# Output projection of both mixers in three rounded products per tile, with the splitting of its weights inside the attention

## The chip, the cores and the metric

The kernel runs on one core of a Trainium2 chip. Its time is the device time of one execution in microseconds (us); of several executions the median is given. The profile comes from one execution, and its times are counted from the first instruction in it.

## The reference, cut to what matters

Two decoder layers over 256 tokens of width 1024. Each layer has a token mixer (layer 0: sparse attention in three branches with gates; layer 1: causal block attention), a residual with LayerNorm, a mixture of 16 experts (top 2 of one group of 4), and a residual with LayerNorm again. The change touches the product with `w_out` at the end of each mixer:

```
def nsa_mixer(h, w_in, w_out, ...):
    proj = h @ w_in
    ...
    o = g[:, :, 0] * heads(o_cmp) + g[:, :, 1] * heads(o_slc) + g[:, :, 2] * heads(o_win)
    return o.reshape(B, S, D_MODEL) @ w_out          # (256 x 1024) @ (1024 x 1024)

def moba_mixer(h, w_in, w_out):
    ...
    o = lax.map(chunk, jnp.arange(S // QB))
    return _merge_chunks(o) @ w_out

for layer in range(2):
    mix = nsa_mixer(x, ...) if layer == 0 else moba_mixer(x, ...)
    x = layer_norm(DN_ALPHA * x + mix, ...)
    x = layer_norm(DN_ALPHA * x + grouped_moe(x, ...), ...)
```

All of it is fp32. The kernel has two ways to multiply at that precision: a plain fp32 matmul, or three matmuls in fp32r (a rounded fp32), in which each factor is split into its rounded value (hi) and the rest (lo), and hi x hi, hi x lo and lo x hi are added up.

## The kernel before, in words

Each engine has its own program, and semaphores tie them together. The weights stream from memory by SyncE's queue into `ring`, eight slots of 128 x 4096 fp32 (2 MiB each); a ninth place is `extra`, a part of `R56`. A slot is loaded anew when TensorE has used what was in it.

**Projections** (`project`, lines 478 to 498, and `split_hi`, `split_lo`). A unit of weights is 1024 x 512, in one slot, cut into eight chunks of 128 x 512, j = 0 to 7. For each chunk ScalarE casts it to fp32r (line 901, into `wh`), VectorE subtracts that from the chunk (line 1155, into `wl`), and TensorE does three fp32r matmuls for each of the two token tiles a (lines 492 to 494). `xh` and `xl` hold the split input.

**Attention** (`attention`, lines 596 to 614) goes by items m, 16 in layer 0 and 8 in layer 1; an odd item has 256 keys for each query, an even one 128. One item passes from engine to engine: TensorE's scores (lines 525, 529, 534), VectorE's maximum (`attention_max`, line 1204), ScalarE's four exponentials with their sums (line 1027), VectorE's coefficient (`coefficients`, line 1237 and in layer 0 also 1242), GpSimd's scaling of the probabilities (line 1100), TensorE's transposes (line 548), VectorE's copy of them out of PSUM (line 1419), TensorE's product with the values (`times_v`, line 564), and after every second item VectorE's copy of the output into `OT` (line 1428 in layer 0, 1430 in layer 1). The order on each engine is written out by hand: VectorE's loop (lines 1410 to 1430) does in turn the maximum of item m, the coefficient of m-1, the copy of the transposes of m-2, and in odd turns from m = 5 on the copy to `OT`. TensorE's does the scores of m, the transposes of m-2 and the values of m-3. ScalarE does the exponentials of m (lines 1018 to 1030), GpSimd the scaling of m (lines 1098 to 1100).

**Output projection** (`mix_out`, lines 616 to 627). The two units of `w_out`, w = 0 and 1, lie in two ring slots. Each of 8 chunks j, 2 token tiles a and 2 units w is one fp32 matmul of 128 x 128 by 128 x 512, 32 in each layer; in the profile an fp32 matmul is two MATMUL records, so line 623 has 128. The order is (a, w) = (0,0), (0,1), (1,0), (1,1). The first six of (0,0) stand before the values of the last item, the others behind. The residual was put into the PSUM banks before (`seed`, line 630). After (0,1) comes the LayerNorm of token tile 0 on VectorE, beside TensorE's (1,0); in the middle of (1,1) stand the logits of the router (line 636). SyncE waits with the next expert loads for (1,0) and (1,1), which free the slots of `w_out`.

**Experts** (`experts`, lines 713 to 764) are fp32 matmuls against weights from the ring (lines 678 and 699), pair by pair; they keep SyncE's queue full.

Of the kernel before, what the change touches and what calls it, by code (L numbers as in the profile page):

```python
# [15 lines left out]
P = 128  # L16
D, S = 1024, 256
T = S // P
# [72 lines left out]
def build(nc, x, consts, w_in0, w_out0, cmp_kw1, cmp_kw2, cmp_vw1, cmp_vw2, cmp_kpos, cmp_vpos,  # L91
          w_in1, w_out1, router_w, router_b, w_gate, w_up, w_down, ln_g, ln_b, out):
    ctx = ExitStack()
    with ctx:
        def sb(name, shape, dt=F32):
            return ctx.enter_context(nc.sbuf_tensor(name, shape, dt))

        def sem(name):
            return ctx.enter_context(nc.semaphore(name))


        ring = sb("ring", [P, SLOT, KJ * UNIT])
        wh = sb("wh", [P, WBUF, UNIT], F32R)
        wl = sb("wl", [P, WBUF, UNIT], F32R)
# [1 line left out]
        X = sb("X", [P, T, D])  # L106
        xh = sb("xh", [P, KJ, S], F32R)
        xl = sb("xl", [P, KJ, S], F32R)
        R2 = sb("R2", [P, T * D])
        R3 = sb("R3", [P, T * D])  # L110
        R4 = sb("R4", [P, T * D])
        R56 = sb("R56", [P, 6 * D])
        R5, R6 = R56[:, 0:3 * D], R56[:, 3 * D:6 * D]
        extra = R56[:, 2 * D:6 * D]
        small = sb("small", [P, 832])
# [18 lines left out]

        qT = R2[:, :].rearrange("p (j t) -> p j t", j=KJ)
        OT = [R6[:, 1536 + j * S:1536 + (j + 1) * S] for j in range(6)] + [R5[:, 2560 + j * S:2560 + (j + 1) * S] for j in range(2)]
        OT2 = [R6[:, 1536 + u * 512:2048 + u * 512] for u in range(3)] + [R5[:, 2560:3072]]
        xTr = R3[:, :].rearrange("p (j t) -> p j t", j=KJ)
        Xp = [v[:, :, :].rearrange("p j t -> p (j t)").rearrange("p (a j c) -> p a j c", a=T, j=KJ) for v in (xh, xl)]
# [61 lines left out]
        landed = [[sem(f"landed{s}_{h}") for h in range(2)] for s in range(SLOT + 1)]  # L201
        w_hi, w_lo, w_used = sem("w_hi"), sem("w_lo"), sem("w_used")
        cmpw_used = sem("cmpw_used")
        bconst = sem("bconst")
        out_done = sem("out_done")
        padded, round_over = sem("padded"), sem("round_over")
# [15 lines left out]
        def ready(k, t, w):  # L222
            return 2 * (k * T + t) + w + 1
# [43 lines left out]
        def in_slot(what):  # L267
            n = SLOT_OF[AT[what]]
            return ring[:, n] if n < SLOT else extra

        def landing(what, h):
            c = AT[what]
            n = sum(1 for b in range(c + 1) if SLOT_OF[b] == SLOT_OF[c] and (h == 0 or in_halves(STREAM[b])))
            return landed[SLOT_OF[c]][h], 16 * n
# [49 lines left out]
        def out_of(l, u, b):  # L324
            return ps[:, 6 + u % 2, 0:S] if l == 0 else ps[:, 6 + u % 2, b * S:(b + 1) * S]


        block = ctx.enter_context(nc.Block())

# [136 lines left out]
        def _(pe):  # L466
# [148 lines left out]

            def mix_out(l, a, w, js):
                B, u = base[l], OUT[2 * l + w]
                for j in js:
                    if a == 0 and w == 0:
                        pe.wait_ge(L.ot_sb, B.ot_sb + j + 1)  # L620
                    if a == 0 and j % 4 == 0:
                        pe.wait_ge(*landing(("unit", u), j // 4))
                    last = mm(ps[:, 2 * a + w, :], OT[j][:, a * P:(a + 1) * P],  # L623
                              in_slot(("unit", u))[:, j * UNIT:(j + 1) * UNIT],
                              start=False, stop=(j == KJ - 1), skip_group_check=True)
                if j == KJ - 1:
                    last.then_inc(L.mix, 1)

# [260 lines left out]
        def _(act):  # L889
# [67 lines left out]
            for l in range(2):  # L957
# [60 lines left out]
                for m in range(n):  # L1018
                    act.wait_ge(L.mx, B.mx + m + 1)
                    if m >= 2 and m % T == 0:  # L1020
                        act.wait_ge(L.pt, B.pt + m - 1)
                    if m >= 4 and m % T:
                        act.wait_ge(L.pt, B.pt + m - 3)
                    k = (m % T + 1) * P
                    for a in range(2):
                        for b in range(2):
                            last = nc.scalar.activation(probs(m)[:, a, b], ps[:, 2 * (m % T) + a, b * k:(b + 1) * k], ACT.Exp,  # L1027
                                                        bias=nmax[:, m % 2, a, b:b + 1],
                                                        accum_out=sums[:, m % 3, a, b:b + 1])
                    last.then_inc(L.exp, 1)  # L1030
                    if l == 0 and m == 1:
                        act.wait_ge(c_less, 1)
                        nc.scalar.activation(Pc, Pc, ACT.Exp).then_inc(c_exp, 1)
                def rows_hi(a, w):
                    c = slice(64 * w, 64 * w + 64)
                    act.wait_ge(N.x_ready, ready(2 * l, a, w))
                    copy(Xp[0][:, a, :, c], X[:, a].rearrange("p (c j) -> p j c", j=KJ)[:, :, c]).then_inc(R.xp, 1)

                for a in range(T):
# [17 lines left out]
        def _(pool):  # L1057
# [29 lines left out]
            for l in range(2):  # L1087
# [10 lines left out]
                for m in range(ITEMS[l]):  # L1098
                    pool.wait_ge(L.coef, B.coef + m + 1)
                    tt(probs(m), probs(m), bc(coef[:, m % 3], 3, (m % T + 1) * P), ALU.mult).then_inc(L.scaled, 1)  # L1100
                for k in (2 * l, 2 * l + 1):
                    for t in range(T):
                        pool.wait_ge(N.stats, k * T + t + 1)
                        tt(rstd[:, t:t + 1], ve[:, t:t + 1], half[:, t:t + 1], ALU.pow).then_inc(N.rstd, 1)
                        if k == 2 * l:
                            for w in range(2):
                                c = slice(64 * w, 64 * w + 64)
                                pool.wait_ge(R.xp, C.xp + 2 * t + w + 1)
                                tt(Xp[1][:, t, :, c], X[:, t].rearrange("p (c j) -> p j c", j=KJ)[:, :, c],
                                   Xp[0][:, t, :, c], ALU.subtract).then_inc(R.xl, 1)  # L1110
                    if k == 2 * l:
                        pool.wait_ge(R.table, C.table + 1)
                        experts(l)
                        pool.wait_ge(R.over, C.over + 1)
                        most = pool.value_load(over[0:1, 0:1], min_val=0, max_val=S)
                        with pool.If(most > SLOTS):
                            pool.wait_ge(main.comb, 2 * T * PAIRS * (l + 1))
                            with pool.Fori(0, ROUNDS - 1) as rho:
                                spare_round(spare[l], rho)
                                pool.wait_ge(spare[l].comb, 2 * T * PAIRS * (rho + 1))  # L1120
                                pool.sem_inc(round_over, 1)
# [3 lines left out]
        def _(dve):  # L1125
# [245 lines left out]
            for l in range(2):  # L1371
# [38 lines left out]
                for m in range(n + 4):  # L1410
# [10 lines left out]
                        compressed_scale()  # L1421
                    if l == 0 and m == 3:
                        compressed_copy()
                    if m >= 4 and m % T:
                        dve.wait_ge(L.pv, B.pv + m - 3)
                        u = (m - 4) // T
                        if l == 0:
                            copy(OT[u], ps[:, 6 + u % 2, 0:S]).then_inc(L.ot_sb, 1)
                        else:
                            copy(OT2[u], ps[:, 6 + u % 2, :]).then_inc(L.ot_sb, 2)  # L1430
                half_stats(0, 0, 0, L.mix, B.mix + 1)
                step(half_stats(0, 1, 0, L.mix, B.mix + 2))
                layer_norm(2 * l, 0, 0, L.ln_in, B.ln_in + 32)
# [63 lines left out]
```

## Time and profile before

| | us |
|---|---|
| median of 3 runs | 785.61 (784.04 to 785.99) |
| the profiled execution, its time | 782.36 |
| the profiled execution, its span | 780.6 |
| attention of layer 0, first score to last product with the values | 87.4 to 153.8 |
| output projection of layer 0 | 146.7 to 178.9 |
| experts of layer 0 | 194.1 to 399 |
| projections of layer 1 | 412.8 to 486.5 |
| attention of layer 1 | 487.2 to 521.4 |
| output projection of layer 1 | 514.9 to 547.4 |
| experts of layer 1 | 562.6 to 767 |

A profile lists per engine the instructions, their start and length, and what ended the idle time before them. PE is TensorE's matmuls, PEld its weight loads (which overlap matmuls), DVE is VectorE, ACT ScalarE, POOL GpSimd, SPq SyncE's issue of transfers. A row of the timeline is: start, length, engine, line, operation, out<-in, shapes, count, and in brackets the idle time before it and who ended it. Lengths of rows that follow each other overlap a little; what an instruction costs in a full stream is the distance of starts.

### The profile page before, as it was taken

The page shows a single profiled execution, that of the slowest core. Times are in us where ns is not written, and L with a number is a line of the kernel's source. Part 1 is how long each engine was busy: PE and PEld are TensorE (multiplying, and loading weights), DVE is VectorE, ACT ScalarE, POOL GpSimd, SP SyncE. Part 2 cuts the span into 40 slices and gives each one's busy share as a digit, 9 for nine tenths or more (in the row PEclk, how much of TensorE's full clock was granted, in tenths as well). Part 3 has the DMA queues.
Part 4 walks back from the last instruction along what each step waited for, and adds up shares of the span by engine and source line. Part 5 has one row for each costly group of instructions (what it writes and reads, how often), then busy time and mean ns, then how long its engine had stood idle before and what let it go on. Part 6 is the DMA issues. An engine that isn't in the chain of part 4 may idle for free.

```text
span 780.6 us, 8983 instructions
## 1 busy us (share of the span) xinstructions
PE 738.4 (95%) x3717; PEld 389.7 (50%) x3717; DVE 289.0 (37%) x537; ACT 179.1 (23%) x412; POOL 84.7 (11%) x72
## 2 busy tenths in 40 slices
PE   5999999998999999999978999899899999999994
PEld 4877755555334443443337887555534344434331
DVE  3584576327112211221155874633611221212125
ACT  3443655022011101110114455602201110111000
POOL 0011244112000000000000320411200000000000
PEclk9999999999999999999987999999999999999998
DMA  9999600127899999999999964112699999999991
GB/s 297 366 387 402 276 1 2 55 98 279 312 403 430 427 428 429 429 424 420 422 390 387 374 216 165 52 55 107 270 363 406 430 427 427 427 427 428 423 420 76
DMA packets 41228, 245.04 MB, mean 314 GB/s; under 512 B 5600, under 2 KB 9824, under 8 KB 26848
## 3 DMA queue, kind: packets, MB, share of 16 engines
q1 hardware_dynamic: 41184, 244.41, 77.9%
q8 instruction: 32, 0.52, 0.3%
q14 instruction: 12, 0.10, 0.0%
HBM read 243.35 MB, written 1.05 MB: 313 GB/s over the span
## 4 chain that ended last, share of the span: by engine, by line
PE 79%; DVE 8%; DMA 8%; issue 2%; ACT 1%; POOL 0%; SPq 0%; DVEq 0%
PE ps L678 24%; PE ps L699 13%; PE ps L623 7%; DMA ring<-in_w_up 7%; PE ps L492 5%; PE ps L493 5%; PE ps L494 5%; PE ps L663 3%; PE ps L709 3%; PE ps L564 2%; PE ps L654 1%; PE ps L630 1%; PE ps L548 1%; PE ps L475 1%; DVE R L1419 1%
## 5 line engine op out<-in xcount | busy, mean ns | idle before, releaser
L678 PE MATMUL ps<-ring,R 128*64 128x512 f32 x928 | 227.1, 595 | 0.0
L678 PEld LDWEIGHTS ps<-ring,R 128*64 128x64 f32 x928 | 70.1, 137 | 108.6 <-issue 106.7
L699 PE MATMUL ps<-ring,R 128*64 128x512 f32 x448 | 113.5, 596 | 0.0
L1155 DVE TENSOR_TENSOR wl<-ring,wh 128x512 fp32r<-128x512 f32 x88 | 66.5, 769 | 49.9 <-ACT wh L901 49.7
L923 ACT ACTIVATE wh<-ps,small 128x512 fp32r<-128x512 f32 x32 | 22.0, 688 | 263.4 <-PE ps L699 261.9
L492 PE MATMUL ps<-wh,xh 128*128 128x512 f32 x176 | 72.4, 412 | 5.0 <-DVE wl L1155 4.9
L493 PE MATMUL ps<-wl,xh 128*128 128x512 f32 x176 | 71.2, 404 | 0.0
L494 PE MATMUL ps<-wh,xl 128*128 128x512 f32 x176 | 71.0, 404 | 0.0
L699 PEld LDWEIGHTS ps<-ring,R 128*64 128x64 f32 x448 | 35.1, 137 | 67.0 <-issue 63.9
L901 ACT CAST wh<-ring 128x512 fp32r<-128x512 f32 x88 | 54.2, 621 | 59.8 <-PE ps L494 59.8
L1323 DVE SCALAR_TENSOR_TENSOR wl<-ps,small,wh 128x512 fp32r<-128x512 f32 x32 | 24.0, 751 | 104.8 <-ACT wh L923 104.1
L623 PE MATMUL ps<-ring,R 128*128 128x512 f32 x128 | 56.8, 597 | 0.9 <-DVE R L1430 0.9
L1312 DVE TENSOR_TENSOR R<-R,ps 128x512 f32<-128x512 f32 x16 | 17.1, 1070 | 104.0 <-PE ps L678 104.0
L1319 DVE TENSOR_SCALAR wl<-ps 128x256 fp32r<-128x256 f32 x16 | 6.8, 425 | 106.7 <-PE ps L684 106.7
L1027 ACT ACTIVATE R<-ps,small 128x128 f32<-128x128 f32 (+1 forms) x96 | 39.1, 419 | 29.3 <-DVE small L1204 29.1
L678 PE MATMUL ps<-R 128*64 128x512 f32 x96 | 42.9, 596 | 1.7 <-DMA ring<-in_w_up 1.7
L1100 POOL TENSOR_TENSOR R<-R,small 128x512 f32<-128x512 f32 (+1 forms) x24 | 35.2, 1468 | 61.9 <-DVE small L1242 33.6
L492 PEld LDWEIGHTS ps<-wh,xh 128*128 128x128 f32 x176 | 34.1, 194 | 15.0 <-DVE xl L1150 4.8
L1067 POOL TENSOR_TENSOR R<-wh,small 128x512 f32<-128x512 f32 x8 | 8.4, 1044 | 282.8 <-PE ps L684 271.7
L494 PEld LDWEIGHTS ps<-wh,xl 128*128 128x128 f32 x176 | 34.0, 193 | 8.5
L623 PEld LDWEIGHTS ps<-ring,R 128*128 128x128 f32 x128 | 23.7, 190 | 28.6 <-issue 26.9
L493 PEld LDWEIGHTS ps<-wl,xh 128*128 128x128 f32 x176 | 34.0, 193 | 7.8
(157 smaller groups left out, 828.7 us busy)
## 6 DMA issues: line engine op xcount, KB each, us to landing
ring<-in_w_gate SPq DMA_DIRECT2D x28, 2048.0 KB, 17.0
ring<-in_w_up SPq DMA_DIRECT2D x22, 2048.0 KB, 17.8
ring<-in_w_down SPq DMA_DIRECT2D x22, 2048.0 KB, 19.4
ring<-in_w_in SPq DMA_DIRECT2D x22, 1024.0 KB, 14.0
ring<-in_w_down SPq DMA_DIRECT2D x12, 1024.0 KB, 26.3
ring<-in_w_out SPq DMA_DIRECT2D x8, 1024.0 KB, 14.7
R<-in_w_up SPq DMA_DIRECT2D x4, 2048.0 KB, 17.6
ring<-in_w_up SPq DMA_DIRECT2D x8, 1024.0 KB, 15.7
```

The lines of the kernel that those rows point to most:

```text
L492: mm(to, xh[:, j, tok], wh[:, c % WBUF], start=(j == 0), stop=False)
L493: mm(to, xh[:, j, tok], wl[:, c % WBUF], start=False, stop=False)
L494: last = mm(to, xl[:, j, tok], wh[:, c % WBUF], start=False, stop=(j == KJ - 1))
L623: last = mm(ps[:, 2 * a + w, :], OT[j][:, a * P:(a + 1) * P], in_slot(("unit", u))[:, j * UNIT:(j + 1) * UNIT], start=False, stop=(j == KJ ...
L663: last = mm(ps[:, bank, at * n:(at + 1) * n], Xp[k][:, a, j, :], Pm[:, a].rearrange("p e c -> p (e c)")[:, 0:n], start=(a == 0 and k == 0) ...
L678: last = mm(ps[64 * e:64 * e + 64, to, :], xe[:, j, at + 64 * e:at + 64 * e + 64], slots[e][:, j * UNIT:(j + 1) * UNIT], start=(j == 0), s ...
L699: last = mm(ps[64 * e:64 * e + 64, 2 + w, :], hT[:, k, 64 * e:64 * e + 64], slots[e][:, at:at + UNIT], start=(k == 0), stop=(k == FJ - 1))
L901: copy(wh[:, c % WBUF], in_slot(("unit", u))[:, j * UNIT:(j + 1) * UNIT]).then_inc(w_hi, 1)
L1027: last = nc.scalar.activation(probs(m)[:, a, b], ps[:, 2 * (m % T) + a, b * k:(b + 1) * k], ACT.Exp, bias=nmax[:, m % 2, a, b:b + 1], accu ...
L1100: tt(probs(m), probs(m), bc(coef[:, m % 3], 3, (m % T + 1) * P), ALU.mult).then_inc(L.scaled, 1)
L1155: tt(wl[:, c % WBUF], in_slot(("unit", u))[:, j * UNIT:(j + 1) * UNIT], wh[:, c % WBUF], ALU.subtract).then_inc(w_lo, 1)
L1323: stt(Yp[1][w], ps[:, 2 + w, :], slot_gate, Yp[0][w], ALU.mult, ALU.subtract).then_inc(rd.y_lo, 1)
```

## The change

28 of the 32 products of each layer's output projection (j = 0 to 6) are done as three fp32r matmuls each; j = 7 stays one fp32 matmul. For this

- ScalarE casts the 14 chunks of `w_out` into `WO_HI`, that is into `xh`, `xl`, `wh` and `wl`, which are free after the projections. It does so right behind the exponentials of an item: one chunk behind each of the items 1 to 14 in layer 0, two behind each of the items 1 to 7 in layer 1 (`wo_chunks`).
- The rest is written over the chunk in its ring slot (a second tensor at the same address, `slot_r`). GpSimd does all 14 in layer 0 and the even ones in layer 1, behind the scaling of the same item; VectorE does the odd ones in layer 1, in the turn of the same item.
- VectorE writes `OT` split: a copy that rounds, a wait for it, and a subtraction.
- TensorE waits ahead of the first product for all rests.
- ScalarE's first cast of the new x for the experts (`rows_hi`) waits for (1,0), since it writes `xh`.

```diff
@@ -95,10 +95,21 @@
+        def sb_twice(name, shape):
+            with nc.sbuf_tensor(name + "_r", shape, F32R) as rounded:
+                pass
+            return sb(name, shape), rounded
+
         def sem(name):
+        slot_r = []
+        for n in range(SLOT):
+            with ExitStack() as room:
+                if n:
+                    room.enter_context(nc.sbuf_tensor(f"below_slot{n}", [P, n, KJ * UNIT], F32))
+                slot_r.append(room.enter_context(nc.sbuf_tensor(f"slot{n}_r", [P, KJ * UNIT], F32R)))
         ring = sb("ring", [P, SLOT, KJ * UNIT])
@@ -106,10 +117,10 @@
         xl = sb("xl", [P, KJ, S], F32R)
-        R2 = sb("R2", [P, T * D])
+        R2, R2r = sb_twice("R2", [P, T * D])
         R3 = sb("R3", [P, T * D])
         R4 = sb("R4", [P, T * D])
-        R56 = sb("R56", [P, 6 * D])
+        R56, R56r = sb_twice("R56", [P, 6 * D])
         R5, R6 = R56[:, 0:3 * D], R56[:, 3 * D:6 * D]
@@ -134,6 +145,15 @@
         OT = [R6[:, 1536 + j * S:1536 + (j + 1) * S] for j in range(6)] + [R5[:, 2560 + j * S:2560 + (j + 1) * S] for j in range(2)]
+        R5r, R6r = R56r[:, 0:3 * D], R56r[:, 3 * D:6 * D]
+        OT_HI = [R6r[:, 1536 + j * S:1536 + (j + 1) * S] for j in range(6)] + [R5r[:, 2560:2560 + S]]
+        OT_LO = [R2r[:, j * S:(j + 1) * S] for j in range(7)]
+        OT2_HI = [R6r[:, 1536 + u * 512:2048 + u * 512] for u in range(3)]
+        OT2_LO = [R2r[:, u * 512:(u + 1) * 512] for u in range(3)]
+        flat = [v[:, :, :].rearrange("p j t -> p (j t)").rearrange("p (n c) -> p n c", c=UNIT) for v in (xh, xl)]
+        WO_HI = [[flat[0][:, 0], flat[0][:, 1], flat[1][:, 0], flat[1][:, 1], wh[:, 0], flat[0][:, 2], flat[0][:, 3]],
+                 [flat[1][:, 2], flat[1][:, 3], wh[:, 1], wh[:, 2], wl[:, 0], wl[:, 1], wl[:, 2]]]
+        WO = [(w, j) for w in range(2) for j in range(KJ - 1)]
         OT2 = [R6[:, 1536 + u * 512:2048 + u * 512] for u in range(3)] + [R5[:, 2560:3072]]
@@ -201,6 +221,7 @@
         cmpw_used = sem("cmpw_used")
+        wo_hi, wo_lo, wo_lo_dve = sem("wo_hi"), sem("wo_lo"), sem("wo_lo_dve")
         bconst = sem("bconst")
@@ -324,6 +345,13 @@
+
+        def wo_lo_at(l, w, j):
+            return slot_r[SLOT_OF[AT[("unit", OUT[2 * l + w])]]][:, j * UNIT:(j + 1) * UNIT]
+
+        def wo_chunks(l, m):
+            per = l + 1
+            return [(n, WO[n]) for n in range(per * (m - 1), per * m) if 0 <= n < len(WO)]
@@ -615,14 +643,23 @@
                 B, u = base[l], OUT[2 * l + w]
+                if a == 0 and w == 0 and js.start == 0:
+                    pe.wait_ge(wo_lo, (14, 21)[l])
+                    if l:
+                        pe.wait_ge(wo_lo_dve, 7)
                 for j in js:
                         pe.wait_ge(L.ot_sb, B.ot_sb + j + 1)
-                    if a == 0 and j % 4 == 0:
-                        pe.wait_ge(*landing(("unit", u), j // 4))
-                    last = mm(ps[:, 2 * a + w, :], OT[j][:, a * P:(a + 1) * P],
-                              in_slot(("unit", u))[:, j * UNIT:(j + 1) * UNIT],
-                              start=False, stop=(j == KJ - 1), skip_group_check=True)
+                    if a == 0 and j == KJ - 1:
+                        pe.wait_ge(*landing(("unit", u), 1))
+                    to, tok = ps[:, 2 * a + w, :], slice(a * P, (a + 1) * P)
+                    if j == KJ - 1:
+                        last = mm(to, OT[j][:, tok], in_slot(("unit", u))[:, j * UNIT:(j + 1) * UNIT],
+                                  start=False, stop=True, skip_group_check=True)
+                    else:
+                        mm(to, OT_HI[j][:, tok], WO_HI[w][j], start=False, stop=False, skip_group_check=True)
+                        mm(to, OT_HI[j][:, tok], wo_lo_at(l, w, j), start=False, stop=False, skip_group_check=True)
+                        last = mm(to, OT_LO[j][:, tok], WO_HI[w][j], start=False, stop=False, skip_group_check=True)
                 if j == KJ - 1:
@@ -1028,12 +1065,17 @@
                     last.then_inc(L.exp, 1)
+                    for n_, (w, j) in wo_chunks(l, m):
+                        act.wait_ge(*landing(("unit", OUT[2 * l + w]), j // 4))
+                        copy(WO_HI[w][j], in_slot(("unit", OUT[2 * l + w]))[:, j * UNIT:(j + 1) * UNIT]).then_inc(wo_hi, 1)
                     if l == 0 and m == 1:
                     act.wait_ge(N.x_ready, ready(2 * l, a, w))
+                    if a == 0 and w == 0:
+                        act.wait_ge(L.mix, B.mix + 3)
                     copy(Xp[0][:, a, :, c], X[:, a].rearrange("p (c j) -> p j c", j=KJ)[:, :, c]).then_inc(R.xp, 1)
@@ -1098,6 +1140,11 @@
                     tt(probs(m), probs(m), bc(coef[:, m % 3], 3, (m % T + 1) * P), ALU.mult).then_inc(L.scaled, 1)
+                    for n, (w, j) in wo_chunks(l, m):
+                        if l == 0 or n % 2 == 0:
+                            pool.wait_ge(wo_hi, len(WO) * l + n + 1)
+                            tt(wo_lo_at(l, w, j), in_slot(("unit", OUT[2 * l + w]))[:, j * UNIT:(j + 1) * UNIT], WO_HI[w][j],
+                               ALU.subtract).then_inc(wo_lo, 1)
                 for k in (2 * l, 2 * l + 1):
@@ -1421,13 +1468,26 @@
                         compressed_copy()
+                    for c, (w, j) in wo_chunks(l, m):
+                        if l and c % 2:
+                            dve.wait_ge(wo_hi, len(WO) * l + c + 1)
+                            tt(wo_lo_at(l, w, j), in_slot(("unit", OUT[2 * l + w]))[:, j * UNIT:(j + 1) * UNIT], WO_HI[w][j],
+                               ALU.subtract).then_inc(wo_lo_dve, 1)
                     if m >= 4 and m % T:
                         u = (m - 4) // T
-                        if l == 0:
+                        if l == 0 and u < 7:
+                            step(copy(OT_HI[u], ps[:, 6 + u % 2, 0:S]))
+                            tt(OT_LO[u], ps[:, 6 + u % 2, 0:S], OT_HI[u], ALU.subtract).then_inc(L.ot_sb, 1)
+                        elif l == 0:
                             copy(OT[u], ps[:, 6 + u % 2, 0:S]).then_inc(L.ot_sb, 1)
+                        elif u < 3:
+                            step(copy(OT2_HI[u], ps[:, 6 + u % 2, :]))
+                            tt(OT2_LO[u], ps[:, 6 + u % 2, :], OT2_HI[u], ALU.subtract).then_inc(L.ot_sb, 2)
                         else:
-                            copy(OT2[u], ps[:, 6 + u % 2, :]).then_inc(L.ot_sb, 2)
+                            step(copy(OT_HI[6], ps[:, 6 + u % 2, 0:S]))
+                            tt(OT_LO[6], ps[:, 6 + u % 2, 0:S], OT_HI[6], ALU.subtract).then_inc(L.ot_sb, 1)
+                            copy(OT[7], ps[:, 6 + u % 2, S:2 * S]).then_inc(L.ot_sb, 1)
                 half_stats(0, 0, 0, L.mix, B.mix + 1)
                 layer_norm(2 * l, 0, 0, L.ln_in, B.ln_in + 32)
```

What moves on VectorE in the attention of layer 1. Before, in the turns of items 3 to 5 (`R` stands for the buffer `R56`, `ps` is PSUM):

```order
L1204 TENSOR_REDUCE small<-ps 128x4 [waits s_done]
L1237 RECIPROCAL small<-small 128x4 [waits exp]
L1419 COPY R<-ps 128x1024 [waits pt]
L1204 TENSOR_REDUCE small<-ps 128x4 [waits s_done]
L1237 RECIPROCAL small<-small 128x4 [waits scaled,exp]
L1419 COPY R<-ps 128x512 [waits pt]
L1204 TENSOR_REDUCE small<-ps 128x4 [waits s_done]
L1237 RECIPROCAL small<-small 128x4 [waits scaled,exp]
L1419 COPY R<-ps 128x1024 [waits pt]
L1430 COPY R<-ps 128x512 [waits pv]
```

The same turns after the change (`slot_r` is the ring slot, `xh`, `xl` and `wh` hold the cast chunks, `R_r` is `OT` split):

```order
L1251 TENSOR_REDUCE small<-ps 128x4 [waits s_done]
L1284 RECIPROCAL small<-small 128x4 [waits exp]
L1466 COPY R<-ps 128x1024 [waits pt]
L1474 TENSOR_TENSOR slot_r<-ring,xh 128x512 [waits wo_hi]
L1251 TENSOR_REDUCE small<-ps 128x4 [waits s_done]
L1284 RECIPROCAL small<-small 128x4 [waits scaled,exp]
L1466 COPY R<-ps 128x512 [waits pt]
L1474 TENSOR_TENSOR slot_r<-ring,xl 128x512 [waits wo_hi]
L1251 TENSOR_REDUCE small<-ps 128x4 [waits s_done]
L1284 RECIPROCAL small<-small 128x4 [waits scaled,exp]
L1466 COPY R<-ps 128x1024 [waits pt]
L1474 TENSOR_TENSOR slot_r<-ring,wh 128x512 [waits wo_hi]
```

A subtraction that waits for ScalarE's cast now stands between one item's turn and the next item's maximum.

ScalarE, the same layer, items 1 and 2 after the change; before, the rows of line 1070 are not there and the exponentials follow each other:

```order
L1064 ACTIVATE R,small<-ps,small 128x256 [waits mx]
L1064 ACTIVATE R,small<-ps,small 128x256 x3
L1070 CAST xh<-ring 128x512 [waits landed2_0] x2
L1064 ACTIVATE R,small<-ps,small 128x128 [waits pt,mx]
L1064 ACTIVATE R,small<-ps,small 128x128 x3
L1070 CAST xl<-ring 128x512 [waits landed2_0] x2
```

The casts of an item come behind its exponentials, which wait (`mx`) for that item's maximum.

## Rows read from the trace of the kernel before

**Rows 1.** The chain of waits in order of time: start, length, what
```profile
513.51 0.87 PE ps L548 x8
514.98 5.35 PE ps L623 x12
...
725.77 27.78 DMA ring<-in_w_up
```
**Rows 2.** Timeline of PEld, output projection of layer 0, the first and last of 32
```profile
155.11 0.19 PEld L623 LDWEIGHTS ps<-ring,R 128*128 128x128 f32 x1 [0.24 <-issue]
...
168.41 0.19 PEld L623 LDWEIGHTS ps<-ring,R 128*128 128x128 f32 x1 [0.24 <-issue]
```
**Rows 3.** Timeline of PE, projections of layer 1, the first and last of 35
```profile
429.67 0.39 PE L492 MATMUL ps<-wh,xh 128*128 128x512 f32 x1
...
437.60 0.39 PE L493 MATMUL ps<-wl,xh 128*128 128x512 f32 x1
```
**Rows 4.** Timeline of DVE, attention of layer 1, items 1, 5, 6 and 7
```profile
489.69 1.23 DVE L1204 TENSOR_REDUCE small<-ps 128x4 f32<-128x1024 f32 x1 [0.70 <-PE ps L534]
...
500.82 1.22 DVE L1204 TENSOR_REDUCE small<-ps 128x4 f32<-128x1024 f32 x1 [1.65 <-PE ps L534]
...
503.15 0.68 DVE L1430 COPY R<-ps 128x512 f32<-128x512 f32 x1
503.75 0.68 DVE L1204 TENSOR_REDUCE small<-ps 128x4 f32<-128x512 f32 x1
...
509.70 0.18 DVE L1237 RECIPROCAL small<-small 128x4 f32<-128x4 f32 x1 [0.20 <-ACT R L1027]
```
**Rows 5.** Timeline of ACT: two rows of the projections, then exponentials of items 5 and 6
```profile
475.39 0.62 ACT L901 CAST wh<-ring 128x512 fp32r<-128x512 f32 x1
475.91 0.59 ACT L914 COPY R<-ps 128x512 f32<-128x512 f32 x1
...
502.08 0.47 ACT L1027 ACTIVATE R<-ps,small 128x256 f32<-128x256 f32 x1 [2.02 <-DVE small L1204]
...
503.80 0.22 ACT L1027 ACTIVATION_READ_ACCUMULATOR R<-ps,small 128x1 f32 x1
504.47 0.37 ACT L1027 ACTIVATE R<-ps,small 128x128 f32<-128x128 f32 x1 [0.45 <-DVE small L1204]
...
505.76 0.21 ACT L1027 ACTIVATION_READ_ACCUMULATOR R<-ps,small 128x1 f32 x1
```
**Rows 6.** Timeline of POOL: scaling of item 7, and two casting subtractions
```profile
509.95 1.90 POOL L1100 TENSOR_TENSOR R<-R,small 128x1024 f32<-128x1024 f32 x1 [1.05 <-DVE small L1237]
...
551.85 3.05 POOL L1109 TENSOR_TENSOR xl<-X,xh 128x512 fp32r<-128x512 f32 x2 [2.60 <-ACT xh L1037]
```
**Rows 7.** Timeline of DVE and of POOL at one place in layer 1's projections
```profile
445.89 0.68 DVE L1155 TENSOR_TENSOR wl<-ring,wh 128x512 fp32r<-128x512 f32 x1
446.78 1.48 DVE L1155 TENSOR_TENSOR wl<-ring,wh 128x512 fp32r<-128x512 f32 x1 [0.22 <-ACT wh L901]
...
446.04 1.67 POOL L1092 TENSOR_TENSOR R<-R 128x512 f32<-128x512 f32 x1 [2.49 <-DVE R L1198]
```
**Rows 8.** Timelines of POOL, PE and DVE, attention of layer 0
```profile
126.45 1.04 POOL L1100 TENSOR_TENSOR R<-R,small 128x512 f32<-128x512 f32 x1 [2.25 <-DVE small L1242]
128.79 1.90 POOL L1100 TENSOR_TENSOR R<-R,small 128x1024 f32<-128x1024 f32 x1 [1.30 <-DVE small L1242]
132.95 1.04 POOL L1100 TENSOR_TENSOR R<-R,small 128x512 f32<-128x512 f32 x1 [2.26 <-DVE small L1242]
...
131.24 1.09 PE L548 MATMUL ps<-cst,R 128*128 128x128 f32 x8
...
98.28 0.69 DVE L1224 TENSOR_TENSOR R<-R,small 128x512 f32<-128x512 f32 x1
```
**Rows 9.** Windows: stretch, length, busy PE, PEld, DVE, ACT, POOL, granted clock, DMA
```profile
486.50:496.50 10.00, 6.95 (x59) 4.53 (x60) 5.01 (x9) 7.62 (x29) 3.61 (x3) 1.00 0.38 162
402.00:418.00 16.00, 8.92 (x28) 7.09 (x29) 12.47 (x23) 4.52 (x8) 1.10 (x2) 0.60 1.05 387
```

## Prediction

> **What bounds the kernel now.** First the page's list of engines: TensorE (PE) is busy nearly throughout, VectorE (DVE), ScalarE (ACT) and GpSimd (POOL) less than half of the time. Then the chain of waits in order of time. It runs through PE in both output projections, each fp32 product behind the one before, and enters them from the transposes of the last item and the values of the one before it (513.51 to 514.98) [rows 1]. From there it goes on through LayerNorm and the experts, and near the end it is a transfer of `in_w_up`, 27.78 us from issue to landing [rows 1]. That transfer looks like a bound of its own, but the queue ahead of it was filled by SyncE each time PE freed a slot. If PE reaches the experts earlier or later, the whole train of transfers shifts with it. So a microsecond before the experts counts in full, in either layer.
>
> Third, the timelines by engine inside the attention of layer 1, since there the change puts its new work. To be seen is who is ahead of whom: the maximum of item 6 starts on DVE at 503.75 [rows 4], while ACT is still in the exponentials of item 5, whose last record starts at 503.80 [rows 5]. The turns of the items overlap: DVE starts the next item before ACT has finished the last.
>
> **Term 1, the products.** A plain fp32 product costs two records. 31 steps of the weight loads take 168.41 - 155.11 = 13.30 us, 0.429 each, 0.858 a product [rows 2]. The fp32r matmul of the same shape, from the same kinds of place, takes 34 steps in 437.60 - 429.67 = 7.93 us, 0.2332 each, 0.700 for three [rows 3]. 56 products (28 in each layer) save 0.158 us each: **-8.8 us**. They lie back to back on PE, which sets the end there; the wait of ACT's first cast for (1,0) delays the transposed x by some 0.6 us, which four products of (1,1) (2.8 us) stand in front of, so it costs nothing.
>
> The Trainium skill ("TensorE: Matmul & The Clock Gate", Back-to-back issue gap) gives 512/2.4 + 2.5 = 216 ns for such a matmul. By an estimate from that page the three would take 0.648 us and the forecast would be 2.9 us lower; the row, 0.2332 us, decides.
>
> **Term 2, the wait in layer 1's attention.** In turn m DVE now waits for the two casts of the same item m, which ACT does behind the exponentials of m, which wait for DVE's maximum of m. DVE's next maximum is queued behind that wait. The turns can no longer overlap. One turn becomes:
>
> - Even item: 0.72 from the start of the maximum to the exponentials (503.75 to 504.47) [rows 4, 5]; 1.39 until ACT can start the next thing (504.47 to 0.10 past 505.76) [rows 5]; two casts 0.52 + 0.62 = 1.14 [rows 5]; 0.03 to DVE; the subtraction, as line 1155, 0.61 as a step of 0.68 [rows 7]. Sum 3.89.
> - Odd item: 1.26 (500.82 to 502.08), 1.82 (502.08 to 0.10 past 503.80), 1.14, 0.03, 0.61: 4.86 [rows 4, 5, 7].
> - In the turns of items 5 and 7 the copy to `OT`, 0.60 as a step (503.15 to 503.75) [rows 4], becomes a copy, a wait and a subtraction of the same size, 1.35: 6.2 in place of 4.86.
>
> To this comes POOL. A subtraction of DVE with both inputs in SBUF took 1.48 in place of 0.68 when POOL was in a long operation: it ended at 448.26, 0.55 after POOL's end at 447.71 [rows 7]. So I take it that DVE waits for POOL there. In an even turn POOL starts the scaling of the item before it, an odd one, about 0.85 after the maximum's start, for 1.90, and then its own new subtraction, for which I take 1.5 (half of 3.05 for two of that kind) [rows 6]. It ends 4.3 after the maximum's start, DVE's subtraction 0.55 later: 4.85 in place of 3.89. In an odd turn POOL's scaling is 1.04 [rows 8] and it is done by 3.95, before DVE comes.
>
> From the maximum of item 1 at 489.69 [rows 4] that makes 2 x 4.86 + 3 x 4.85 + 2 x 6.2 = 36.7 us to the coefficient of item 7, at 526.4. Before, it was at 509.70 [rows 4]. Then come the scaling, from 526.6 for 1.90 [rows 6], and PE's transposes and values, 1.47 before (513.51 to 514.98 [rows 1]) and some 0.1 to get to them: the output projection starts at 530.1 in place of 514.98. Before, PE took up the last transposes at 513.51, 1.66 behind the end of the scaling (509.95 + 1.90), since it was busy with `seed`; that room is why 16.7 late becomes **+15.2 us**. POOL's last subtraction ends at 530.0, just in time. The bounds: without the waiting for POOL 3 x 0.96 less, 12.3; POOL's subtraction at 1.67, as a two-input one took [rows 7], gives some 0.5 more, 15.7.
>
> The Trainium skill ("GPSIMD Engine Reference", Specifications) says that POOL shares its SBUF interfaces with DVE and contends with it where DVE has two SBUF inputs; the trace agrees (1.48 against 0.68). The same skill page (Elementwise — side-by-side cycle accounting) gives 2.6 cycles for an element of two inputs at 1.2 GHz. An estimate from it is 1.1 us for 512, by which term 2 would be some 1.2 us smaller; I keep the trace's 1.5.
>
> **Term 3, the attention of layer 0.** There DVE does not wait for casts, PE is busy nearly throughout, and the new work must fit beside it. Two items take 6.50 us (126.45 to 132.95 [rows 8]). ACT has room: exponentials of two items 3.2 and two casts 1.2. POOL gets 2 x 1.5 to its 1.04 + 1.90 (5.94 in all), and DVE's split of `OT` is some 0.5 us in front of the next maximum. The scaling of an odd item ends at 130.69 and PE takes it up at 131.24 [rows 8]: 0.55 us of room, which the 0.5 just uses up. At the start there is no such room: DVE's two-input operation of the compressed branch at 98.28 [rows 8] comes when POOL, done with scaling item 1 at 98.1, would start its first subtraction; it would wait about 1.4. I take 1.4 + 0.4 for small slips: **+1.8 us**, bounds 0 (all fits) and 4 (0.3 in each of seven periods on top).
>
> **Sum.** -8.8 + 15.2 + 1.8 = +8.2. The profiled execution took 782.36 for a span of 780.6, and would take 790.6; the median of the runs shown is 785.61, 3.25 above it, and would be **793.8 us**, 1.0% slower. A measurement can tell about 0.3% (2.4 us) from no change.
>
> **Rivals.**
> *Slower still, by the clock.* PE's work in layer 1's attention does not grow while the stretch does: it falls from 69% busy (6.95 of 10.00, at granted clock 1.00) to near 58%. In another stretch with 8.92 of 16.00 busy (56%), one with a long idle time in it, the granted clock was 0.60 [rows 9], which is 1.2 GHz in part of it. Inside the attention a halved clock hardly matters (scores wait only for the item two before), but at its end transposes, values (1.6 us) and the first two microseconds or so of products would take twice as long: +3.5, 797.3. For: 56% is near 58%. Against: no long idle time, gaps of 2 us only. Chance 0.22.
> *Faster.* DVE's wait costs nothing, since DVE idles ahead of the maxima anyway (1.65 before item 5's [rows 4]), and ACT before its exponentials (2.02 [rows 5]), which is more than two casts. This decides if exponentials and casts of an item end before DVE would take up the next maximum in any case. Then -8.8 + 1.8: 778.6. Against: the exponentials alone end after the next maximum's start (503.80 and on, against 503.75) [rows 4, 5]. Chance 0.07.
> *Near nothing.* The turns overlap in part by something I misread, and about half of term 2 is paid: -8.8 + 7.6 + 1.8, 786.2. Chance 0.05.
> *The change doesn't do what it says.* The order shows three fp32r matmuls for j = 0 to 6; only their price could fail. If mixing weights of two kinds made them as dear as fp32, term 1 is gone: 802.6. With other mishaps 0.06.
> My forecast has the remaining 0.60.
>
> **How the numbers follow.** The range goes from 789 (no waiting for POOL, layer 0 free: 785.6 - 8.8 + 12.3 = 789.1) to 800 (793.8 + 2.2 for layer 0 + 3.5 for the clock, 799.5). Outside lie the cases faster, near nothing and mishaps, 0.18. Faster 0.07, within 0.3% 0.05, slower 0.88.
>
> **What would show it.** In the profile after: DVE's subtraction of line 1474 idle before for 1 to 2.5 us in each of 7 turns, ended by ACT's cast of line 1070; maxima of layer 1 some 4.9 us apart and 6.2 behind item 5's, in place of 2.9; seven of DVE's subtractions with three near 1.5 us in place of 0.69; products of lines 660 to 662 at 0.233 us; layer 0's experts 2.5 us earlier, layer 1's 8 later. Wrong: maxima 3 us apart with PE ahead of them, products of 0.28 us, or the period of layer 0's attention well above 6.50.

## The result, and the profile after

The changed kernel took 792.49 us (median of 4 runs, 791.12 to 793.91), the kernel before in the same session 785.66. The ratio is 1.0091, 95% interval 1.0067 to 1.0115: slower by 0.9%. The profiled execution took 791.12, for a span of 789.3, against 782.36 and 780.6.

The products took what was expected. TensorE's weight loads in layer 0's output projection, 18 steps apart:

```profile
156.91 0.19 PEld L662 LDWEIGHTS ps<-xl,R_r 128*128 128x128 f32 x1
...
161.09 0.19 PEld L662 LDWEIGHTS ps<-wl,R_r 128*128 128x128 f32 x1
```

4.18 us for 18 steps is 0.2322 us for each fp32r matmul, 0.697 for the three of a product, where the fp32 product took 0.858 [rows 2]. The whole output projection goes, in layer 0, from 148.99 to the first row behind it at 176.56 (27.57 us; before, from 146.72 to 178.80, 32.08), and in layer 1 from 527.50 to 555.49 (27.99; before, 514.91 to 547.29, 32.38). That is 4.5 and 4.4 us less. These are the ends, from TensorE's timeline (the last row is the first behind (1,1)):

```profile
148.99 0.50 PE L660 MATMUL ps<-xh,R_r 128*128 128x512 f32 x1
...
176.56 0.29 PE L680 MATMUL ps<-small,cst 128*128 128x16 f32 x2
...
527.50 0.50 PE L660 MATMUL ps<-xh,R_r 128*128 128x512 f32 x1
...
555.49 0.29 PE L680 MATMUL ps<-small,cst 128*128 128x16 f32 x2
```

The loss is in layer 1's attention. VectorE's timeline there, items 1 to 4 and the end; it answers to [rows 4]:

```profile
488.19 1.22 DVE L1251 TENSOR_REDUCE small<-ps 128x4 f32<-128x1024 f32 x1 [0.70 <-PE ps L562]
489.34 0.17 DVE L1284 RECIPROCAL small<-small 128x4 f32<-128x4 f32 x1
492.44 0.69 DVE L1474 TENSOR_TENSOR slot_r<-ring,xh 128x512 fp32r<-128x512 f32 x1 [2.94 <-ACT xh L1070]
493.05 0.68 DVE L1251 TENSOR_REDUCE small<-ps 128x4 f32<-128x512 f32 x1
493.65 0.17 DVE L1284 RECIPROCAL small<-small 128x4 f32<-128x4 f32 x1
493.74 0.66 DVE L1466 COPY R<-ps 128x512 f32<-128x512 f32 x1
496.33 1.24 DVE L1474 TENSOR_TENSOR slot_r<-ring,xl 128x512 fp32r<-128x512 f32 x1 [1.94 <-ACT xl L1070]
497.49 1.21 DVE L1251 TENSOR_REDUCE small<-ps 128x4 f32<-128x1024 f32 x1
...
502.34 0.68 DVE L1251 TENSOR_REDUCE small<-ps 128x4 f32<-128x512 f32 x1
...
523.70 0.17 DVE L1284 RECIPROCAL small<-small 128x4 f32<-128x4 f32 x1
```

The maxima used to wait for TensorE's scores, all but that of item 6; now only those of items 0 and 1 do (line 1251). From then on the idle time stands in front of the subtraction (line 1474), and what ends it is ScalarE's cast (line 1070): 2.94 us in item 1's turn, then 1.94 in even turns and 1.83 in odd ones. No later maximum has any idle time of its own: the next turn starts when the subtraction is done, or the split of `OT` behind it. Turns are 4.86 us (items 1 and 3), 4.44 (even items) and 6.24 (items 5 and 7). ScalarE, in turn, idles in front of the exponentials, until VectorE's maximum has come:

```profile
491.27 1.15 ACT L1070 CAST xh<-ring 128x512 fp32r<-128x512 f32 x2
493.77 0.37 ACT L1064 ACTIVATE R<-ps,small 128x128 f32<-128x128 f32 x1 [1.36 <-DVE small L1251]
...
495.15 1.15 ACT L1070 CAST xl<-ring 128x512 fp32r<-128x512 f32 x2
```

Each waits for the other, and neither is busy throughout: from 491 to 496 VectorE worked for 1.96 us and ScalarE for 3.64. The chain of waits in this attention went through all four engines before, and stayed on TensorE from 506.55 us on; now it goes round between ScalarE and VectorE:

```profile
495.27 1.03 ACT xl L1070 x2
496.33 1.24 DVE slot_r L1474
497.57 1.15 DVE small L1251
498.74 1.93 ACT R L1064 x8
```

From the maximum of item 1 to the first product it is 527.50 - 488.19 = 39.31 us, and was 514.91 - 489.69 = 25.22: **14.1 us more**. I use this stretch for layer 1 below, and for layer 0 the one from the first maximum (88.54 before, 89.86 after) to the first product: 58.18 before, 59.13 after, 0.95 more. What lies before the first maximum is the same work in both kernels and moved by up to 1.5 us between executions (88.44 to 89.94 over the profiles of all kernels here).

### The profile page after: what moved, and what is told of

The parts are those of the page before. It is cut to its first block, busy times and chain, and to the rows that moved or that the text cites. A ratio compares the mean times of both kernels' runs of the same rounds, so it can differ in the third digit from the quotient of the medians.

```text
span 789.3 us, 9164 instructions
## 1 busy us (share of the span) xinstructions
PE 735.5 (93%) x3773; PEld 403.6 (51%) x3773; DVE 301.3 (38%) x556; ACT 193.3 (24%) x440; POOL 110.8 (14%) x93
## 4 chain that ended last, share of the span: by engine, by line
PE 76%; DVE 9%; DMA 8%; ACT 3%; issue 3%; SPq 0%; POOL 0%; DVEq 0%
PE ps L715 24%; PE ps L736 12%; DMA ring<-in_w_up 7%; PE ps L520 5%; PE ps L521 5%; PE ps L522 5%; PE ps L700 3%; PE ps L746 3%; PE ps L660 2%; PE ps L661 2%; PE ps L662 2%; ACT R L1064 1%; PE ps L592 1%; PE ps L503 1%; PE ps L691 1%
## 5 line engine op out<-in xcount | busy, mean ns | idle before, releaser
L1134 POOL TENSOR_TENSOR R<-R 128x512 f32<-128x512 f32 (+1 forms) x16 | 23.3, 1460 | 126.2 <-DVE R L1245 126.2
L576 PE MATMUL ps<-cst,R 128*128 128x128 f32 x144 | 23.2, 303 | 12.5 <-POOL R L1142 10.7
## 6 DMA issues: line engine op xcount, KB each, us to landing
ring<-in_w_in SPq DMA_DIRECT2D x22, 1024.0 KB, 14.1
```

## The experiments

The first four put the question: is it VectorE's wait for the same item's casts, or the amount of new work, and in which layer? Beside these four the kernel before took 785.17 us, beside the other four 784.78; ratios are to that. "Changed kernel" is the kernel after the change.

**One turn later.** In VectorE's loop:

```diff
-                    for c, (w, j) in wo_chunks(l, m):
+                    for c, (w, j) in wo_chunks(l, m - 1):
```

> The change, but VectorE subtracts its chunk of an item (layer 1) in the turn of the next item, so that it never waits for the casts of the item whose turn it is in. All the work stays. Theory (the turns of layer 1 became serial by that wait): the maxima of layer 1 come about 3 us apart again (ScalarE's exponentials and casts, 2.5 and 3.0 us in turn, or GpSimd's 5.5 us for two items, are then the longest), the output projection of layer 1 starts 2 to 4 us later after the first maximum than before, not 14, and the time is 780 to 783 us, below the kernel before. Rival (the added work itself is too much for ScalarE or GpSimd, whoever waits): the maxima stay above 4 us apart and the time is 788 to 793 us.

Measured: 782.18 us, ratio to before 0.9954 (0.9936 to 0.9971). All the work is still there, and a slower kernel has become a faster one. The stretch of layer 1 is 28.03 us, 2.8 over before, where it was 14.1 over. So the wait was 11.3 us of the loss. What is left shows in VectorE's timeline, here from item 2 to item 4:

```profile
493.68 1.67 DVE L1474 TENSOR_TENSOR slot_r<-ring,xh 128x512 fp32r<-128x512 f32 x1 [0.28 <-ACT xh L1070]
495.27 1.21 DVE L1251 TENSOR_REDUCE small<-ps 128x4 f32<-128x1024 f32 x1
...
497.60 0.67 DVE L1474 TENSOR_TENSOR slot_r<-ring,xl 128x512 fp32r<-128x512 f32 x1
498.20 0.68 DVE L1251 TENSOR_REDUCE small<-ps 128x4 f32<-128x512 f32 x1
...
499.51 2.30 DVE L1474 TENSOR_TENSOR slot_r<-ring,xh 128x512 fp32r<-128x512 f32 x1
```

VectorE is full now, without idle time from 493.68 us to the end of the last subtraction at 516.27, and four of its seven subtractions take 1.67 to 2.30 us. GpSimd's timeline beside them:

```profile
492.90 1.90 POOL L1142 TENSOR_TENSOR R<-R,small 128x1024 f32<-128x1024 f32 x1 [1.06 <-DVE small L1284]
494.75 1.72 POOL L1146 TENSOR_TENSOR slot_r<-ring,xh 128x512 fp32r<-128x512 f32 x1
...
499.37 1.89 POOL L1142 TENSOR_TENSOR R<-R,small 128x1024 f32<-128x1024 f32 x1
```

The subtraction that began at 493.68 ended at 495.35, 0.55 after GpSimd's scaling (494.80); that of 499.51 ended at 501.81, 0.55 after 501.26. And GpSimd's own subtraction, begun while VectorE's ran, takes 1.72 in place of 1.27: it waits too.

**One layer at a time.** In `wo_chunks`, `if l != 0: return []` (or `l != 1`), with the plain products and copies kept for the other layer.

> The change in layer 0 alone; layer 1 as before. Theory: the products of layer 0 save 4.4 us and the attention of layer 0 loses 1: 782.2 us, 0.996 of before. Rival (layer 0 pays as much as it saves, and layer 1 loses less than I say): within 0.1% of before, 785 to 786 us.

> The change in layer 1 alone; layer 0 as before. Theory: +14.1 for the attention and -4.4 for the products: 795.4 us, 1.012 of before. Rival (half of the loss lies in layer 0): 790 us.

Measured: layer 0 alone 781.59, ratio 0.995 (0.9933 to 0.9967); layer 1 alone 794.82, ratio 1.0121 (1.0102 to 1.0139). The stretches are 59.14 (layer 0) and 25.21 (layer 1) in the first, 39.32 (layer 1) in the second: each layer behaves as it does in the whole change, and 785.17 - 3.58 + 9.65 = 791.2 comes within 1.3 us of it. The rivals, which put half of the loss in layer 0, are out. The same change is a gain in one layer and a loss in the other, for in layer 0 nobody in the loop of the maxima waits for a cast.

**The two engines swapped.** VectorE takes the even chunks (cast first) and GpSimd the odd ones:

```diff
-                        if l == 0 or n % 2 == 0:
+                        if l == 0 or n % 2:
-                        if l and c % 2:
+                        if l and c % 2 == 0:
```

> The change, but in layer 1 VectorE subtracts the chunk that ScalarE casts first, and GpSimd the one cast second. VectorE still waits in the turn of the same item, but for one cast and not for two. Theory (the wait for the casts stands in the loop of the turns): each of the 7 turns is shorter by one cast, 0.55 to 0.62 us, 3.9 to 4.3 us in all: 788.4 us. Where GpSimd's subtraction, now later, runs beside that of VectorE, up to half of that is lost. Rival (the length of a turn is set by ScalarE's or GpSimd's work and not by VectorE's wait): no change to the changed kernel, 792 us.

Measured: 790.75 us, ratio 1.0076 (1.0057 to 1.0095). That is 1.7 us below the changed kernel, but the two intervals overlap, so the reading rests on the trace: the stretch is 37.24, 2.1 shorter. The four odd turns each fell by 0.52 us, one cast, the first from 4.86 to 4.34 (487.94 to 492.28). The three even ones stayed at 4.44, since there VectorE now came sooner while GpSimd, in its own subtraction, was no earlier done (3.97 us after the maximum in both kernels):

```profile
491.67 0.69 DVE L1474 TENSOR_TENSOR slot_r<-ring,xh 128x512 fp32r<-128x512 f32 x1 [2.42 <-ACT xh L1070]
492.28 0.68 DVE L1251 TENSOR_REDUCE small<-ps 128x4 f32<-128x512 f32 x1
...
495.04 1.76 DVE L1474 TENSOR_TENSOR slot_r<-ring,xl 128x512 fp32r<-128x512 f32 x1 [1.42 <-ACT xl L1070]
496.72 1.21 DVE L1251 TENSOR_REDUCE small<-ps 128x4 f32<-128x1024 f32 x1
```

Counted from the maximum, it came 0.52 earlier (2.76 against 3.28) and the subtraction was 0.52 longer. Somewhat under half of the gain was lost that way, as the expectation allowed.

**GpSimd out of the way.** Its seven subtractions of layer 1 stand behind the scaling of item 7:

```diff
-                    for n, (w, j) in wo_chunks(l, m):
+                    for n, (w, j) in (wo_chunks(l, m) if l == 0 else enumerate(WO) if m == 7 else []):
```

> The change, but GpSimd does its seven subtractions of layer 1 behind the scaling of item 7 instead of one behind each item. VectorE's waits stay as they are. To be read is the distance of the maxima. Theory (VectorE's subtraction of two SBUF inputs stands still while GpSimd is in an operation): the even turns, 4.44 us in the changed kernel, go down to the 3.89 us that I predicted without GpSimd, VectorE's subtraction there takes 0.69 us and not 1.24, the odd turns stay at 4.86. Rival (the 1.24 us has another cause, such as the cast that ScalarE has just finished): 4.44 stays. The time is no aim here: seven subtractions of 1.27 us stand behind the last scaling, about 798 us.

Measured (one execution): 797.27 us. The first turns:

```profile
492.40 0.68 DVE L1251 TENSOR_REDUCE small<-ps 128x4 f32<-128x512 f32 x1
...
495.68 0.69 DVE L1474 TENSOR_TENSOR slot_r<-ring,xl 128x512 fp32r<-128x512 f32 x1 [1.94 <-ACT xl L1070]
496.29 1.22 DVE L1251 TENSOR_REDUCE small<-ps 128x4 f32<-128x1024 f32 x1
```

The even turn is 3.89 us, the odd one 4.85 (496.29 to the next maximum at 501.14), the subtraction 0.69. So what made it 1.24 us in the changed kernel was GpSimd's operation beside it.

**All on VectorE, one turn later.** The first experiment, with GpSimd's condition `l == 0` and VectorE's `l`.

> The first experiment (subtractions one turn later in layer 1), with all 14 subtractions of layer 1 on VectorE, none on GpSimd. In the first experiment VectorE was busy throughout, and four of its subtractions took 1.67 to 2.30 us beside GpSimd. Theory (they waited for GpSimd's subtraction): seven more steps of 0.61 us (4.3) and 5 us of waiting gone, so about the same, 781.5 to 783 us, with no subtraction above 1.3 us except beside a scaling. Rival (a subtraction here costs VectorE 1.5 to 2 us for another reason): all even turns get another 1.5 us, 787 us or more.

Measured: 785.32 us, ratio 1.0002 (0.9984 to 1.0019), a miss by 2.3 us. The stretch is 31.23 us. Waiting did not go:

```profile
493.58 2.63 DVE L1474 TENSOR_TENSOR slot_r<-ring,xh 128x512 fp32r<-128x512 f32 x2
...
500.92 2.02 DVE L1474 TENSOR_TENSOR slot_r<-ring,wh 128x512 fp32r<-128x512 f32 x1
502.86 0.68 DVE L1474 TENSOR_TENSOR slot_r<-ring,xh 128x512 fp32r<-128x512 f32 x1
```

GpSimd's scaling of an odd item, 1.89 us, starts at 500.50, right behind the coefficient, and VectorE's first subtraction of that turn starts 0.4 later: 1.34 us of waiting, in each of the four even turns. I had blamed GpSimd's subtraction. It was its scaling, which no division of the chunks takes away; so most of the seven added steps (4.3 us in all) was paid, 3.2 us of it in the stretch.

**The rest at the end.** If a subtraction of VectorE must neither wait for a cast nor meet GpSimd, it belongs behind the attention, and half of `w_out` is not needed until (0,1):

```diff
+                    for c, (w, j) in enumerate(WO):
+                        if l and (m == 9 and 7 <= c < 12 or m == 11 and c >= 12):
...
+                if l and a == 0 and w == 1 and js.start == 0:
+                    pe.wait_ge(wo_lo_dve, 7)
```

GpSimd takes the chunks of w = 0, one behind each item. The second run also has GpSimd's subtractions of layer 0 one item later, `wo_chunks(l, m - 1)`.

> The change, but in layer 1 GpSimd subtracts the seven chunks of w = 0, one behind each item from 1 to 7, and VectorE the seven of w = 1 behind the attention, five while TensorE does the first products of (0,0) and two after the last copy to OT; TensorE waits for these only ahead of (0,1). In the turns VectorE has nothing new but the split of OT. Theory: maxima 2.8 to 3.0 us apart, output projection of layer 1 0.5 to 1.0 us later after the first maximum than before (25.2), perhaps 0.5 us of waiting ahead of (0,1): 2 us less than the first experiment, 779.5 to 780.5 us, ratio 0.993. Rival (ScalarE's 14 casts set the pace as soon as VectorE does not): 3.3 us or more a turn, 782 us or more.

> As the run before it, and in layer 0 GpSimd's subtractions come one item later (behind items 2 to 15), so that none of them stands beside VectorE's operation of the compressed branch, which took 1.65 us in place of 0.69. Theory (that operation is the whole loss of layer 0's attention, 0.95 us): it takes 0.69 again and the time is 0.9 us below the run before it, 778.6 to 779.6 us. Rival (the loss comes from the work added in the regular turns, or the last subtraction now delays the first product): the same as the run before it or up to 1 us above.

Measured: 780.38 us, ratio 0.9929 (0.9905 to 0.9952), and 779.41, ratio 0.9918 (0.9895 to 0.9941). VectorE's timeline in the first of the two, at the end of layer 1's attention:

```profile
515.01 1.22 DVE L1466 COPY R<-ps 128x1024 f32<-128x1024 f32 x1 [3.12 <-PE ps L576]
516.15 0.68 DVE L1480 CAST R_r<-ps 128x512 fp32r<-128x512 f32 x1
516.94 0.69 DVE L1481 TENSOR_TENSOR R_r<-ps,R_r 128x512 fp32r<-128x512 f32 x1
517.54 1.28 DVE L1489 TENSOR_TENSOR slot_r<-ring,xl 128x512 fp32r<-128x512 f32 x2
...
522.14 1.28 DVE L1489 TENSOR_TENSOR slot_r<-ring,wl 128x512 fp32r<-128x512 f32 x2
```

All seven take 0.6 a step while TensorE is in (0,0). The last ends at 523.42, and TensorE starts (0,1) at 523.48 with no idle time before it: just in time. The stretch is 26.79 us, 1.6 over before and not 0.5 to 1.0. Half of that was there at item 7's maximum, and the largest piece of it is the step from item 2 to item 3, 3.74 us (490.69 to 494.43) against 2.77 before. The other 0.8 us arises behind item 7's maximum: from there to the first product it is 9.22 us, and was 8.44. By the windows of this run (columns as in [rows 9]) TensorE had the lower of its two levels there, 1.2 GHz, for most of four microseconds (granted 0.55 and 0.60):

```profile
492.00:494.00 2.00, 2.00 (x10) 1.25 (x10) 0.68 (x2) 2.00 (x9) 1.82 (x1) 0.55 0.00 0
494.00:496.00 2.00, 2.00 (x12) 1.53 (x12) 1.31 (x2) 1.67 (x5) 1.49 (x3) 0.60 0.00 0
```

and the scores of item 3 took 2.08 us where they take 1.13. It had idled 0.55 and 0.94 us in the three microseconds before, as in the first experiment, where the granted clock stayed at 1.00. In the second run the granted clock fell too, and that step was 3.93 us. Why it fell in these two executions and not there stays open. The profiled execution of the first run was the slowest of its six, 782.46 us.

The two medians are 0.97 us apart, which by itself is not clear of their intervals; the trace shows that the second run did what was expected in layer 0. The operation of the compressed branch in this run, and in the changed kernel:

```profile
98.17 0.69 DVE L1271 TENSOR_TENSOR R<-R,small 128x512 f32<-128x512 f32 x1
```

```profile
99.59 1.65 DVE L1271 TENSOR_TENSOR R<-R,small 128x512 f32<-128x512 f32 x1
```

In the run before it this operation took 1.65 too. The maximum of item 3, right behind it, starts 10.34 us after the first maximum, 11.32 in the run before it, 11.30 in the changed kernel and 10.35 in the kernel before; up to item 2's maximum all four agree (6.64 or 6.65). The whole stretch is 58.17, as before the change (58.18): the one collision was the whole loss there. This is the best kernel of the study, 0.8% below the kernel before and 1.7% below the changed one.

## Why the prediction was right

The forecast was 793.8 us, in a range of 789 to 800; measured was 792.49, slower. Step by step:

- **Term 1, the products, -8.8.** Measured -4.5 and -4.4, -8.9 together. The fp32r price, taken from the projections [rows 3], was 0.2332 and is 0.2322 here. The 216 ns that the Trainium skill gives as the gap of a single matmul of 512 columns ("TensorE: Matmul & The Clock Gate", Back-to-back issue gap) was not reached in either place; by it the term would have been 2.9 us larger, and the trace disagrees. No cost shows for adding up fp32 and fp32r matmuls in one bank.
- **Term 2, the wait, +15.2.** Measured +14.1, and the first experiment, which takes that wait away and leaves all the work in place, gave back 11.3 of it. The odd turn was predicted as 4.86 and was 4.86; that of item 5 was predicted as 6.2 and was 6.24. The even turn was 4.44 and not 4.85: the mis-sized part is GpSimd's subtraction, for which I took 1.5 us, half of a pair [rows 6], and which took 1.27. It started at 495.75 and ended at 497.02 (below), and VectorE's was over 0.55 later, at 497.57, just as at the place in [rows 7]. Of the 0.41 us, 0.23 are that length, 0.08 that the next maximum starts so much before the row's end, the rest roundings. Three even turns, 1.2 us, are the whole miss of the term. Without GpSimd the sum of the pieces, 3.89, was met to the hundredth. An estimate of 1.1 us from the Trainium skill's figure for such an operation ("GPSIMD Engine Reference", Elementwise — side-by-side cycle accounting) was low by 0.17, my 1.5 high by 0.23; its rule that the two engines contend (Specifications) the trace bears out (1.24 us against 0.69).

```profile
495.75 1.27 POOL L1146 TENSOR_TENSOR slot_r<-ring,xh 128x512 fp32r<-128x512 f32 x1
```

- **The end of the term.** I had the transposes of the last item wait for GpSimd, with 1.66 us of TensorE's room used up. They did:

```profile
525.89 1.09 PE L576 MATMUL ps<-cst,R 128*128 128x128 f32 x8 [1.54 <-POOL R L1142]
```

- **Term 3, layer 0, +1.8.** Measured +0.95. The collision at the compressed branch was there, 0.96 in place of 1.4. Half of that miss is GpSimd's subtraction, 1.29 and not 1.5; the other half is my sum, since 98.1 + 1.5 + 0.55 = 100.15 lies 1.2 us, not 1.4, behind the unhindered end at 98.97 [rows 8]. The further 0.4 for small slips was not there. The period stayed 6.50.
- **What the terms leave.** -8.9 + 14.1 + 0.95 = 6.15 us, where the medians differ by 6.8. In the two profiled executions the difference is 8.76, of which 1.3 us was there before the first maximum of layer 0, ahead of all that the change touches. Of the 1.3 that then remain, 0.7 lies between the output projection of layer 0 and the first maximum of layer 1 (311.63 us against 310.89), and 0.5 behind that of layer 1; where in these stretches it arises was not looked into. The terms together were 2 us too high, and it is luck that the medians differ from the forecast by 1.3 only.
- **The rival of the clock.** The granted clock did fall in layer 1's attention, to between 0.67 and 0.72 in three of the windows of 5 us, with TensorE idle for 2 to 3.4 us ahead of each, as the windows of the changed kernel show:

```profile
491.00:496.00 5.00, 1.94 (x15) 1.05 (x13) 1.96 (x4) 3.64 (x14) 2.10 (x2) 0.94 0.00 0
496.00:501.00 5.00, 4.79 (x38) 3.59 (x40) 3.56 (x4) 2.56 (x10) 3.15 (x3) 0.72 0.00 0
...
516.00:521.00 5.00, 5.00 (x22) 3.27 (x22) 3.57 (x4) 2.56 (x10) 3.15 (x3) 0.67 0.00 0
521.00:527.00 6.00, 4.46 (x34) 2.65 (x34) 2.65 (x5) 0.66 (x2) 3.15 (x3) 1.00 0.00 0
```

  But from 521 on it was 1.00, with 1.54 us of idle time before the last transposes, and the last transposes took 1.09 us as before [rows 1]. So the 3.5 us that the rival put at the end were not paid, and inside the turns VectorE waited for ScalarE, not for TensorE. TensorE's busy share did not fall to 58%: from 491 to 521 it was 21.21 of 30.00 us, 71%, since part of the work took longer at the lower clock.
- **The others.** The faster rival held that the idle time ahead of the maxima covers the wait. It decides when exponentials and casts of an item end before the next maximum would start anyway. They end 3.25 us (even items) or 4.2 (odd) after their maximum's start, and the turns of the kernel before were 2.0 to 3.4 long. The rival near nothing had the turns overlap in part; they did not at all.

## What to carry to other kernels

When an engine's new work consumes what another engine makes from the first one's output of the same turn, a pipelined loop becomes a ring, and its period is the sum of both engines' parts, however much idle time both have; taking the consumer one turn later costs a line and gave back 10 us here. Price new work by where it stands in each engine's order, not by busy shares, and look for a place where nothing is behind it: half of the operand was not needed until (0,1), 8 us after the first product (515.49 to 523.48 in the first run with the rest at the end). And an operation of VectorE with both inputs in SBUF should be placed where GpSimd is idle.

## What the runs showed of the hardware

VectorE and GpSimd held each other up where VectorE had two inputs in SBUF, in both directions. VectorE's 128x512 operation of that kind, 0.69 us alone, ended 0.55 us after GpSimd's operation in each place looked at, so that it took from 1.24 to 2.30 us by when it came. GpSimd's subtraction, 1.27 alone, took 1.72 to 1.77 when it started during VectorE's. Where one of VectorE's inputs was in PSUM no wait showed: in the first experiment the split of `OT` took its 0.69 us while GpSimd was in a subtraction (of 1.77, which had begun during an earlier one of VectorE's from SBUF):

```profile
512.97 0.69 DVE L1486 TENSOR_TENSOR R_r<-ps,R_r 128x512 fp32r<-128x512 f32 x1
```

```profile
511.63 1.77 POOL L1146 TENSOR_TENSOR slot_r<-ring,wh 128x512 fp32r<-128x512 f32 x1
```

TensorE's clock made a microsecond of difference where the instructions were the same. With the change in layer 1 alone, layer 0 is as before, and yet its stretch was 59.21 us and not 58.18. In the windows of that run TensorE had 1.2 GHz for six microseconds (granted 0.50 from 94 to 100), with item 3's scores among them:

```profile
94.00:96.00 2.00, 2.00 (x10) 0.93 (x9) 1.56 (x3) 0.42 (x1) 0.00 (x0) 0.50 0.00 0
...
98.00:100.00 2.00, 2.00 (x8) 0.81 (x5) 1.90 (x6) 0.43 (x3) 0.77 (x1) 0.50 0.00 0
```

In the kernel before it was at most four (0.61 and 0.54 from 94 to 98, 1.00 behind). The scores of item 1 began at 88.69 and 88.67, and those that start at 117.19 in the kernel before start at 118.23 in that run. So a loss of a microsecond is to be read from the operation at which it arises, not from the ends of a stretch of one execution.
